# New order of a layer's attention part, with the second convolution product behind the fourth unit of the sparse attention

## The reference

```python
h = rmsnorm(x, norm_mix[layer]);  z = h @ w_in[layer]
u_glu, q_nsa, kv_nsa, g_nsa, c_q, c_kv, k_rope, g_merge = jnp.split(z, split_at, axis=-1)
y_conv = conformer_conv(u_glu, ...)           # a * sigmoid(b), 31 causal taps, layernorm, silu, @ w_proj
y_nsa = nsa_attention(q_nsa, kv_nsa, g_nsa, ...) @ w_branch_nsa[layer]
y_mla = mla_attention(c_q, c_kv, k_rope, ...) @ w_branch_mla[layer]
g_conv, g_attn, g_mla = jnp.split(sigmoid(g_merge), 3, axis=-1)
x = x + (g_conv * y_conv + g_attn * y_nsa + g_mla * y_mla) @ w_out[layer]
x = x + memory_cross_attention(rmsnorm(x, ...), rmsnorm(mem, ...), ...)
gate, up = jnp.split(rmsnorm(x, norm_ffn[layer]) @ w_gate_up[layer], 2, axis=-1)
x = x + (silu(gate) * up) @ w_down[layer]
```

## Time and profile before

| | us |
|---|---|
| median of 3 runs | 2366.81 |
| lowest, highest | 2362.83, 2367.13 |
| profiled execution | 2365.05 |
| its span | 2363.6 |
| PE busy | 2173.1 (92%) |
| DVE busy | 1399.7 (59%) |
| ACT busy | 1114.2 (47%) |
| mean granted clock of TensorE | 0.955 |

### The profile page before, as it was taken

One profiled execution on the slowest core, in us unless ns is written; L12 is line 12 of the kernel. 1 busy time (PEld: TensorE's weight loads), 2 busy tenths in 40 slices (PEclk: granted clock), 3 DMA queues, 4 the chain that ended last, 5 costly groups with the idle time before them and its releaser, 6 DMA issues.

```text
span 2363.6 us, 25173 instructions
## 1 busy us (share of the span) xinstructions
PE 2173.1 (92%) x9936; PEld 1782.5 (75%) x9936; DVE 1399.7 (59%) x1941; ACT 1114.2 (47%) x1721; POOL 33.4 (1%) x45
## 2 busy tenths in 40 slices
PE   7998888999999888899989999988999999978998
PEld 6776767888787676788878878767788788766886
DVE  4886464655488646465555556665555555566553
ACT  4544444544444443454444445534544444465443
POOL 0000000000000000000000000100000000000000
PEclk9998799999999879999999999999999999998999
DMA  7642133555444213355545544312455454543543
GB/s 223 193 180 86 64 139 118 183 186 188 177 179 168 82 68 138 116 178 188 186 169 178 189 176 177 127 72 91 169 192 181 169 192 181 186 143 118 193 180 125
DMA packets 52804, 369.25 MB, mean 156 GB/s; under 512 B 6191, under 2 KB 6447, under 8 KB 9040
## 3 DMA queue, kind: packets, MB, share of 16 engines
q1 hardware_dynamic: 48960, 356.54, 42.2%
q10 hardware_dynamic: 3216, 9.53, 1.2%
q0 software_dynamic: 512, 1.57, 0.4%
HBM read 366.31 MB, written 1.31 MB: 156 GB/s over the span
## 4 chain that ended last, share of the span: by engine, by line
PE 78%; DVE 15%; ACT 4%; issue 1%; DMA 1%; POOL 0%; ACTq 0%; DVEq 0%
PE ps L435 22%; PE ps L437 22%; PE ps L436 22%; DVE ring_lo L976 4%; DVE acc L1189 3%; PE ps L481 3%; PE ps L531 2%; PE ps L633 1%; PE ps L465 1%; ACT upper_w L1639 1%; PE ps L516 1%; DMA ring<-in_w 1%; ACT z L1696 1%; DVE xn L1114 1%; ACT S L1713 1%
## 5 line engine op out<-in xcount | busy, mean ns | idle before, releaser
L976 DVE TENSOR_TENSOR ring_lo<-ring,upper_w 128x1024 fp32r<-128x1024 f32 x659 | 803.6, 1228 | 519.7 <-ACT upper_w L1639 515.3
L1639 ACT CAST upper_w<-ring 128x1024 fp32r<-128x1024 f32 x659 | 689.4, 1054 | 591.1 <-PE ps L437 572.1
L435 PE MATMUL ps<-upper_w,nT_hi 128*128 128x512 f32 x1992 | 791.0, 397 | 41.4 <-DVE nT_lo L1583 15.5
L436 PE MATMUL ps<-ring_lo,nT_hi 128*128 128x512 f32 x1992 | 779.1, 391 | 0.0
L437 PE MATMUL ps<-upper_w,nT_lo 128*128 128x512 f32 x1824 | 713.2, 391 | 0.0
L435 PEld LDWEIGHTS ps<-upper_w,nT_hi 128*128 128x128 f32 x1992 | 379.6, 191 | 122.8 <-issue 17.6
L436 PEld LDWEIGHTS ps<-ring_lo,nT_hi 128*128 128x128 f32 x1992 | 378.9, 190 | 75.6 <-issue 0.5
L437 PEld LDWEIGHTS ps<-upper_w,nT_lo 128*128 128x128 f32 x1824 | 345.4, 189 | 73.0
L437 PE MATMUL ps<-upper_w,tT_lo 128*128 128x512 f32 (+1 forms) x792 | 308.7, 390 | 0.0
L435 PE MATMUL ps<-upper_w,z_hi 128*128 128x512 f32 x624 | 244.3, 391 | 2.7 <-DVE x L1035 2.7
L436 PE MATMUL ps<-ring_lo,z_hi 128*128 128x512 f32 x624 | 242.8, 389 | 0.0
(11 more groups left out here) (288 smaller groups left out, 1403.6 us busy)
## 6 DMA issues: line engine op xcount, KB each, us to landing
ring<-in_w SPq DMA_DIRECT2D x339, 1024.0 KB, 4.8
big<-in_gains ACTq DMA_DIRECT2D x7, 512.0 KB, 3.7
z<-in_mem ACTq DMA_DIRECT2D x2, 1024.0 KB, 5.4
big<-skew POOLq DMA_DIRECT2D x8, 192.0 KB, 13.4
x<-in_x SPq DMA_DIRECT2D x1, 1024.0 KB, 5.3
xn<-in_w ACTq DMA_DIRECT2D x1, 1024.0 KB, 4.8
out<-x ACTq DMA_DIRECT2D x2, 512.0 KB, 3.1
const<-in_const ACTq DMA_DIRECT2D x1, 529.0 KB, 3.5
```

Of the source, the lines that this page charges most:

```text
L435: PE.matmul(out, hi, w_hi, start=start, stop=False)
L436: PE.matmul(out, hi, w_lo, start=False, stop=False)
L976: V.tensor_tensor(ring_lo[:, q % RING, cols], ring[:, q % RING, cols], upper_w[:, n % AHEAD, :].bitcast(F32), ALU.subtract).then_inc(*lo_c ...
L1639: A.copy(upper_w[:, n % AHEAD, :], ring[:, q % RING, part * HALF:(part + 1) * HALF]).then_inc(*hi_cut.up(h))
```

## The change

`weight_stream` gives the blocks the order 0, 1, 8, 9, 10, 11, 2, 3, 4, 5, then the compression weights, then in6 and in7. Borders now stand before each layer's compression weights alone; behind them one run of halves reaches from in6 to the next layer's in5, or to the end. hyb.dt comes behind hyb.x0.

On PE, neighbouring blocks now alternate between banks 0 and 1 and banks 2 and 3. The turns of queries, keys and token blocks go into in2 and in3, the mean before the last group of the compression product, and the small products of the compression (variance, `hid`, `kc` and `vc`, block scores, block weights, block values) behind single halves of in6 and in7. The parts of `c` are made before the units. conv0 becomes the `first` of the units and writes banks 4 and 5; conv1 goes behind the fourth unit (index 3), uqn behind index 5 and uqp behind index 6. ukv starts the latent attention; nsa0 stands between its turns, and nsa1 alone is `first`. DVE and ACT are written in the matching order: taps of the convolution start in in8, nine follow the last cut of in5; ACT reads in8 and in10 out of PSUM instead of DVE.

`keep_on` is new: matmuls of a constant into a free bank, whose result nobody reads, before the parts of each norm: 1 in a layer's feed-forward net, 9 before ffn_a, 6 each before hyb, ffn_b, ffn_c, rec and ffn_d. In layer 0, POOL issues each of the eight bias DMAs behind the last half of the next block, not all at once.

```diff
+FIRST, LAST = (0, 1, 8, 9, 10, 11, 2, 3, 4, 5), (6, 7)
+
+
 def weight_stream():
     w = Stream()
     for l in range(DEPTH):
         at = l * LAYER_CHUNKS
-        for b in range(12):
+        for b in FIRST:
             w.add(f"{l}.in{b}", [at + 2 * b, at + 2 * b + 1])
-        w.end_run(f"{l}.in0", f"{l}.in11")
+        w.end_run(f"{l - 1}.in{LAST[0]}" if l else "0.in0", f"{l}.in{FIRST[-1]}")
         w.add(f"{l}.cmp", range(at + 24, at + 28), split=False)
+        for b in LAST:
+            w.add(f"{l}.in{b}", [at + 2 * b, at + 2 * b + 1])
         at += 28
...
-        w.end_run(f"{l}.conv0", f"{l}.ffn.down")
...
-    w.add("hyb.dt", [at + 6], halves=1)
+        if b == 0:
+            w.add("hyb.dt", [at + 6], halves=1)
...
-    w.end_run("ffn_a.up0", "ffn_d.down")
+    w.end_run(f"{DEPTH - 1}.in{LAST[0]}", "ffn_d.down")
```

```diff
+        def keep_on(n, b):
+
+            free(b)
+            for i in range(n):
+                PE.matmul(ps[:, b, :], ident, const[:, 0:BLK], start=True, stop=True)
...
+            rows_in(1, (2, 3))
+            rows_in(8, (0, 1))
             turn(f"{l}.u", cols_of(ostage), CONV_CT, [dve_out.at(f"{l}.in1")], lambda c: act_out.at(f"{l}.u.{c}"))
...
+            rows_in(9, (2, 3))
+            rows_in(10, (0, 1))
+            rows_in(11, (2, 3))
+            rows_in(2, (0, 1), {0: queries, 2: keys})
+            rows_in(3, (2, 3), {0: blocks})
+            rows_in(4, (0, 1))
+            rows_in(5, (2, 3))
+
+            def mean():
+                PE.wait_ge(*dve_out.at(f"{l}.tap{CONV_W - 1}.{CONV_CT - 1}"))
+                free(4)
+                for c in range(CONV_CT):
+                    m = PE.matmul(ps[:, 4, 0:T], ones, acc[:, c, :], start=(c == 0), stop=(c == CONV_CT - 1))
+                m.then_inc(*psum_full.up(f"{l}.mu"))
+                held(dve_out.at(f"{l}.mu"), 4)
...
+                    if kind and cc:
+                        mean()
...
+            rows_in(6, (0, 1), {0: hidden, 1: block_rows, 2: block_scores})
+            rows_in(7, (2, 3), {0: block_weights, 1: block_values})
 
         def nsa_attention(l):
+            c_at = parts(f"{l}.c", cols_of(z, Z_CQ), 5, lambda c: (), (6, 7))
...
             def conv_product():
+                gemm(f"{l}.conv0", of_parts(four), (4, 5), [dve_out.at(f"{l}.convT")])
+                held(dve_out.at(f"{l}.conv0"), 4, 5)
...
                 held(dve_out.at(f"{l}.conv1"), 6, 7)
-            attention(nsa_units(l), scores, lambda i: [act_out.at(f"{l}.k.0")] if i == 0 else (), first=conv_product)
```

```diff
+            beside = {3: conv_rest, 5: lambda: latent_queries(f"{l}.uqn", 512, (0, 1), f"{l}.qn"), 6: lambda: latent_queries(f"{l}.uqp", 256, (2, 3), f"{l}.qp")}
+            attention(nsa_units(l), scores, lambda i: [act_out.at(f"{l}.k.0"), act_out.at(f"{l}.q.2")] if i == 0 else (), first=conv_product, beside=beside)
...
+            parts(f"{l}.nsaT", cols_of(ostage), 4, lambda c: [dve_out.at(f"{l}.nsa7.sum")], (6, 7))
+            turn(f"{l}.qnT", cols_of(z, QN), 4, [dve_out.at(f"{l}.qn")], split_evac(f"{l}.qnT"), banks=(2, 3))
+            turn(f"{l}.knT", cols_of(z, KN), 4, [act_out.at(f"{l}.kn")], split_evac(f"{l}.knT"), banks=(4, 5))
+            gemm(f"{l}.nsa0", of_parts(nsa_parts), (6, 7), [dve_out.at(f"{l}.nsaT.lo3")])
+            held(dve_out.at(f"{l}.nsap0"), 6, 7)
...
-                    gemm(f"{l}.nsa{b}", of_parts(nsa_parts), (4 + 2 * b, 5 + 2 * b), [dve_out.at(f"{l}.nsaT.lo3")])
-                    held(dve_out.at(f"{l}.nsap{b}"), 4 + 2 * b, 5 + 2 * b)
-            attention(mla_units(l), scores, lambda i: [dve_out.at(f"{l}.rotT.0"), act_out.at(f"{l}.kpT"), act_out.at(f"{l}.vn")] if i == 0 else (), first=nsa_product)
+                gemm(f"{l}.nsa1", of_parts(nsa_parts), (6, 7))
+                held(dve_out.at(f"{l}.nsap1"), 6, 7)
+            attention(mla_units(l), scores, lambda i: heads_ready if i == 0 else (), first=nsa_product)
...
-            ffn(f"{l}.ffn", lambda c: [dve_out.at(f"{l}.x_xo{c // 4}")])
+            ffn(f"{l}.ffn", lambda c: [dve_out.at(f"{l}.x_xo{c // 4}")], 1)
             for hf in range(2):
                 held(dve_out.at(f"{l}.x_ffn{hf}"), DOWN[0] + hf, DOWN[1] + hf)
-        ffn("ffn_a", lambda c: [dve_out.at(f"final.x{c // 4}")])
+        ffn("ffn_a", lambda c: [dve_out.at(f"final.x{c // 4}")], 9)
```

POOL's part and ACT's order around in6 and in7:

```diff
+            rows_in(6, 0, block_of(z, 4), ACT.Sigmoid, {0: hidden, 1: block_rows, 2: normed, 3: block_weights})
+            rows_in(7, 2, block_of(z, 5), ACT.Sigmoid, {1: weights_turned})
...
+            def conv_product():
+                cuts(f"{l}.conv0")
...
                 G.wait_ge(*skew_stored.at("skew"))
                 for r in range(0, P, 16):
+                    if r:
+                        G.wait_ge(*half_used.at(W.span[f"0.in{FIRST[2 + r // 16]}"][-1]))
                     shifted = bass.AP(skew.tensor, skew.offset + P - 1 - r, [[BLK - 1, 16], [P * BLK, 8], [1, BAND]])
```

587 lines of the change are left out of this document (295 added, 292 removed).

## The result

The changed kernel takes 2322.49 us (median of 4, 2320.05 to 2325.33) beside 2365.15 for the kernel before (median of 4): ratio 0.9819, 95% interval 0.9803 to 0.9835. A second set of 4 executions gave 2323.51. The prediction said 2329, range 2308 to 2348. Its direction and most of its mechanisms held; several of its terms were off by a few microseconds, and one was wrong in kind.

What follows compares the result with a forecast made beforehand. The bound was taken to be a chain of small steps through PE, DVE and ACT; -26.4 for both layers, -2.1, -6.5, -3.5, -1.3, +1.2 and +1.4 sum to -37.2: 2327.9, about 2329 us in a median, range 2308 to 2348.

Steps and rivals of the forecast that it cites:

- 1, banks of in2 and in3: Stretch before the compression: with neighbours alternating banks, the waits before and behind in2 go; -1.9 us per layer.
- 2, compression: Up to the first sparse unit: four waits of 1.7, 3.8, 3.4, 3.4, plus 4.5 for cold gaps; +3.1 us per layer.
- 3, units: Eight sparse units with conv1, uqn and uqp moved in: waits 9.3, cold running 2.4; -3.5 us per layer (0 to -6).
- 4, latent attention: Latent attention with work moved forward, 5.3 still lost before unit 0's values; -10.9 us per layer (-7 to -14).
- 5, entry: Entry to layer 1: in0's three first cuts are made during the down product; -2.1 us.
- 6, bias copies: Layer 0: eight skew copies spread a block apart, where a cast waited 5.20 for a ring load; -6.5 us (-3 to -7.5).
- 7, dummies: Dummy products before norms: five norms -3.5 us together, ffn_a -1.3, both layers' ffn +1.2.
- 8, hyb.dt: hyb.dt goes into block x1, so its 48 small matmuls no longer cover the evacuation of x2; +1.4 us.
- The clock stays up: Rival: cold running in the layers and some short waits do not come; 16 us less, 2312; chance 0.22.
- New waits take the place: Rival: in in6, in7 and the units, four halves per layer pay 2.3 us each; +18, 2347; chance 0.15.
- ACT's casts are named as what DVE waits for in most halves of in6 to ukv: Sign, from in6 to ukv in each layer, that would show the forecast wrong; no size of its own.
- the slower side: Rival: all 34 halves from in6 to ukv in both layers pay 2.3 us each; +78, 2406; chance 0.05.

Runs made afterwards that it cites:

- the three edits: Block weights sooner, latent attention's chain and unit 0's chain reordered in the changed kernel: singly 2309.82, 2306.94 and 2307.02 us, all together 2286.42 us.
- bias_at_once: Changed kernel with layer 0's eight bias DMAs issued together, as before the change: 2318.96 us.
- conv1_first: Changed kernel with conv1 right behind conv0, ahead of the first unit, on all three engines: 2309.55 us.
- latent_chain: Changed kernel with nsa1 written to banks 0 and 1, and DVE and ACT doing unit 0's copy first in the latent attention: 2306.94 us.
- borders_back: Changed kernel with the borders before layer 1 and before ffn_a put back, three casts and cuts made at once there: 2325.01 us.
- the last set: Kernel with block weights sooner, latent chain and unit 0's chain, without the dummy matmuls: 2295.35 us, beside 2286.42 with them.

## Why the prediction was right

**What bounds these stages.** Right: the chain through DVE and ACT, not PE's work. Each of the three edits that only reorder steps (and banks) took 13 to 16 us by the medians and 9 to 14 between traced executions; PE's own work is the same in all.

**1, banks of in2 and in3.** The last stage before the compression holds ten blocks (109.0) and 28 transposes (3.1) in 112.17 us: no wait is left. Right.

**2, compression.** The four waits were right in layer 0 to 0.4 us each (1.58, 3.40, 3.61, 3.45 for 1.7, 3.8, 3.4, 3.4), and sum to 12.0 for 12.3. The step that failed is "three such gaps at 1.5 each make 4.5": only the first was paid in full (4.58 for 3.0). Behind the wait of 3.61 the scores and conv0 ran cold in layer 1 and warm in layer 0:

```profile
189.06 0.58 PE L447 MATMUL ps<-upper_w,nT_hi 128*128 128x512 f32 x1
...
198.34 0.63 PE L534 MATMUL ps<-const,S 128*128 128x128 f32 x4 [3.45 <-DVE rs L1107]
```

```profile
763.21 0.99 PE L447 MATMUL ps<-upper_w,nT_hi 128*128 128x512 f32 x1
...
768.44 2.36 DVE L1025 TENSOR_TENSOR ring_lo<-ring,upper_w 128x1024 fp32r<-128x1024 f32 x2 [2.88 <-ACT upper_w L1701]
770.72 1.22 DVE L1138 TENSOR_TENSOR xn<-ps,z 128x1024 f32<-128x1024 f32 x1
```

conv0 took 7.06 us for 5.83, but the wait for its merge then was 1.82 and not 3.45. The merge (L1138) starts behind DVE's two cuts, which wait for a cast, and these end only when the cold product does (770.80 and 770.27): from the transposes behind the wait of 3.61 to unit 0's transposes it is 11.12 us cold and 11.11 warm. Slow matmuls in front of a wait that another engine sets cost nothing here. The third price, in layer 0, falls behind unit 0's transposes and so into the units (4.71 us up to unit 1's transposes for 3.02 in layer 1). So +1.0 and not +3.1, in both layers.

**3, units.** -2.2 for -3.5: 49.3 us where 48.0 was summed. The waits by the queue had been 9.3 us, and were 1.99, 0.76, 0.24, 1.53, 1.35 and 0.79 in layer 1: about 6.7. They can't be set against the 9.3 as they are, since cold matmuls hide a part of them. The execution at full clock (`bias_at_once`, layer 1) has 1.98, 1.17, 0.76, 0.23, 1.53, 1.35 and 1.22, 8.2 in all, and took 46.35 where the warm sum had 45.6. So the warm sum was 0.7 too low, and the cold price was 3.0 where 2.4 stood. Single waits were further off: 1.35 for the 2.7 of unit 6. What the prediction did not ask is what conv1 does at its new place. It counted 5.5 us of moved work there and 3.4 of waiting for conv0's merge in term 2, and never set the one against the other; `conv1_first` did.

**4, latent attention.** -11.5 for -10.9, with the wait for unit 0's copy at 4.88 for 5.3. Right, and `latent_chain` shows that the wait is DVE's queue.

**5, entry.** -2.8 for -2.1; `borders_back` gives 2.8 up to in0 in the trace, and 1.6 behind it.

**6, bias copies.** The mechanism is right, the size is not: with the copies together again the stage is 3.6 to 3.7 longer, for 6.5. With the new order of the blocks PE then waits 1.69 and 0.92 for two late loads, and a cast that is 5.1 late ahead of them is covered; the prediction took over the whole difference between the old layers. The table's -4.9 is the difference of the layers' gains; what makes up the 1.2 between it and the experiment is open. The sign "the layer 0 cast without a DMA wait" came only in part: one cast still waits 3.58 for the ring, and PE has no wait behind it.

**7, dummies.** Wrong in kind at the step "warm ones then wait 1.0 for the parts". The x of the norm comes in two halves 1.3 apart, so the second group of transposes starts at 1363.22, 1.32 behind the first, and by its end the parts are there: no wait. The first matmul comes 2.2 us behind the start of the transposes, not 2.9. It is 7.6 us by the last set, about 1.5 a norm, for the 3.5 of the sum. The forecast had its row from a layer's norm, where all sixteen transposes start together.

**8, hyb.dt.** +1.4 in the sum. From hyb.x0's first matmul to the state products it is 160.7 us for 159.1 before, although the first matmuls are warm now; so about +2 by estimate, the 1.6 and some 0.5 for the warm start.

**The rivals.** "The clock stays up" did not come in the changed kernel (0.90 and 0.88 in the two stages), but its size is now known: the units at full clock are 3 us shorter, and the three edits brought the latent stage to 1.00. "New waits take the place" did not come for PE, which in the changed kernel waits for a cut only once a layer between in6 and ukv, 1.58 us. But the prediction's own sign against itself, that "ACT's casts are named as what DVE waits for in most halves of in6 to ukv", did come: they are named for 11 of the 17 halves in layer 0 and for 10 in layer 1, with up to 4.25 us. The sign was badly chosen and not the forecast: DVE cuts ahead of PE's use, and a cast that is late for DVE is not yet late for PE. That is why the slower side, which priced such halves at 2.3 us each, was far off.

**The number.** 2329 for 2322.5 is in part luck. In the table, terms that turned out better than forecast sum to 11.3 us and terms that turned out worse to 4.5; what is left is the 6.8 between -37.2 and -44.0.

The four waits came as walked with 1.28 us a table load and nothing behind it. The Trainium skill (ScalarE: Activation LUTs, "What ACT_TABLE_LOAD costs") adds a drain of about 1.38 us, which by the prediction's estimate would have made the sum 8 us worse; the traces decide against it.
